# Scores of 26 expert tiles moved out of the expert loop of a two-block transformer kernel

## The reference, cut to what matters

```python
q = jnp.einsum('td,dhk->thk', x_t, w_q).reshape(T, PEER_HEADS, 2, PEER_HALF)
s = jnp.einsum('thpk,hpnk->thpn', q, sub_keys).astype(jnp.float32)
sv, si = lax.top_k(s, K)
...
fv, fpos = lax.top_k(cand, K)
eidx = jnp.take_along_axis(cidx, fpos, axis=-1)
gate = jax.nn.softmax(fv, axis=-1)
u = u_emb[eidx]
v = v_emb[eidx]
act = jax.nn.gelu(jnp.einsum('thkd,td->thk', u, x_t).astype(jnp.float32), approximate=False)
return jnp.einsum('thk,thkd->td', (gate * act).astype(x_t.dtype), v)
```

## Time and profile before

| | |
|---|---|
| median of 3 runs | 2806.69 us |
| the profiled execution, its span | 2806.97 us, 2804.9 us |
| PE, PEld busy | 2476.3 us (88%), 2096.4 us (75%) |
| DVE, ACT busy | 2020.6 us (72%), 539.7 us (19%) |
| chain that ended last | PE 77%, DVE 15%, issue 3% |
| layer 0: key choice, gate making | 665.8 to 777.7, 777.7 to 887.2 us |
| layer 0: start, experts | 887.2 to 893.8, 893.8 to 1614.3 us |
| layer 1 | the same, 1171 us later (key choice ends at 1948.7) |

### The profile page before, as it was taken

How to read it: one execution, slowest core, us unless ns; L and a number is a source line. 1 busy time by engine, 2 the same in 40 slices (tenths; PEclk the granted TensorE clock), 3 DMA queues, 4 the chain that set the end, 5 groups by cost and what they waited for, 6 DMA issues and landing times.

```text
span 2804.9 us, 40133 instructions
## 1 busy us (share of the span) xinstructions
PE 2476.3 (88%) x13930; PEld 2096.4 (75%) x13930; DVE 2020.6 (72%) x4410; ACT 539.7 (19%) x943; POOL 0.2 (0%) x4
## 2 busy tenths in 40 slices
PE   8977999788467999999999976783789999999998
PEld 6645886455456999999999955462579999999997
DVE  2334344634999888888888754469988888888887
ACT  2322000110133111111111133310321111111111
POOL 0000000000000000000000000000000000000000
PEclk9978999799789999999999988896999999999998
DMA  5323677552100555555555452011025555555553
GB/s 210 126 88 132 242 288 279 216 218 90 46 0 28 190 183 191 182 192 181 193 180 191 160 201 90 31 61 45 0 83 182 192 180 193 181 192 182 190 184 128
DMA packets 87182, 429.05 MB, mean 153 GB/s; under 512 B 10064, under 2 KB 10704, under 8 KB 77008
## 3 DMA queue, kind: packets, MB, share of 16 engines
q1 hardware_dynamic: 87120, 428.23, 43.6%
HBM read 427.14 MB, written 1.05 MB: 153 GB/s over the span
## 4 chain that ended last, share of the span: by engine, by line
PE 77%; DVE 15%; issue 3%; ACT 2%; DVEq 1%; DMA 1%; SPq 0%; ACTq 0%
PE ps L430 53%; PE ps L462 10%; PE ps L452 6%; DVE HN L1464 4%; PE ps L628 2%; PE ps L492 1%; DVEq L1464 1%; PE ps L510 1%; DVE HT L1100 1%; DVE HN L1462 1%; DVE arena L1382 1%; DVE arena L1380 1%; DVE arena L1386 1%; DVE arena L1220 1%; ACT arena L855 1%
## 5 line engine op out<-in xcount | busy, mean ns | idle before, releaser
L430 PE MATMUL ps<-ring_rounded 128*128 128x256 f32 x4096 | 778.4, 283 | 3.6 <-DVE ring_rounded L1482 3.6
L430 PE MATMUL ps<-ring_rounded,HN_rounded 128*128 128x512 f32 x3072 | 744.9, 391 | 1.3 <-DVE HN_rounded L1482 1.3
L430 PEld LDWEIGHTS ps<-ring_rounded 128*128 128x128 f32 x4096 | 656.5, 192 | 13.8 <-DVE ring_rounded L1482 4.0
L430 PEld LDWEIGHTS ps<-ring_rounded,HN_rounded 128*128 128x128 f32 x3072 | 560.6, 188 | 107.8 <-DVE HN_rounded L1482 2.0
L1482 DVE TENSOR_TENSOR ring_rounded<-ring,ring_rounded 128x1024 fp32r<-128x1024 f32 x512 | 625.4, 1222 | 9.0
L430 PE MATMUL ps<-HT_rounded,ring_rounded 128*128 128x256 f32 x2048 | 580.2, 283 | 0.0
L1478 DVE CAST ring_rounded<-ring 128x1024 fp32r<-128x1024 f32 x512 | 352.9, 689 | 213.6 <-DMA ring<-in_experts_u 211.0
L430 PEld LDWEIGHTS ps<-HT_rounded,ring_rounded 128*128 128x128 f32 x2048 | 392.8, 192 | 9.8
L462 PE MATMUL ps<-HT,ring 128*128 128x256 f32 x1472 | 335.7, 389 | 18.6 <-DVEq L1107 18.6
L462 PEld LDWEIGHTS ps<-HT,ring 128*128 128x128 f32 x1472 | 285.5, 196 | 60.8 <-DVEq L1107 20.6
L975 ACT ACTIVATE HN<-ps 128x256 f32<-128x256 f32 x256 | 98.5, 385 | 1169.7 <-PE ps L430 1169.7
(11 more groups left out here) (193 smaller groups left out, 1541.1 us busy)
## 6 DMA issues: line engine op xcount, KB each, us to landing
ring<-in_stream SPq DMA_DIRECT2D x69, 2048.0 KB, 7.7
ring<-in_experts_u SPq DMA_DIRECT2D x256, 512.0 KB, 4.4
ring<-in_experts_v SPq DMA_DIRECT2D x256, 512.0 KB, 3.7
ring<-in_stream SPq DMA_DIRECT2D x2, 1024.0 KB, 7.3
arena<-in_keys SPq DMA_DIRECT2D x2, 1024.0 KB, 14.1
ring<-in_stream SPq DMA_DIRECT2D x1, 1664.0 KB, 8.3
ring<-in_stream SPq DMA_DIRECT2D x1, 1040.0 KB, 19.3
X<-in_x SPq DMA_DIRECT2D x1, 1024.0 KB, 4.9
```

The costliest lines, as they stand in the source:

```text
L430: mm = pe.matmul(out_, p, q, start=(first and i == 0), stop=(last and i == 2))
```

## The change

Of the 128 tiles of each layer, the scores of 26 are computed ahead of the experts, by plain fp32 matmuls on the unsplit HT and u (`early_scores`): 12 behind the last key scores, 2 behind the transposes, and 12 in eighths between the groups of gate making (`gate_steps`: three matmuls in every two groups). Four slots of `ring`, then free, hold their u. ACT applies gelu and keeps the result: 14 tiles (`CHOICE_TILES`) in `early`, in the arena; 12 (`GATE_TILES`) in `meanwhile`, in `ring`. For the 14, the gates are multiplied in at once: behind the one-hots of group g, DVE multiplies the gates of group g-2, straight from PSUM, into `early` (`gate_early`), once ACT has copied the other 114 columns. The buffer of gates shrinks to 114 columns a token. The gates' exponentials and sums are now one step for all heads. The gate loops are written out. The experts begin with 26 tiles of values alone (`early_expert`); the other 102 go as before.

```diff
+P_SLOTS = 4
+CHOICE_TILES, GATE_TILES = 14, 12
+AFTER_CHOICE, AFTER_EXP = 12, 8
+EARLY = CHOICE_TILES + GATE_TILES
+LATE = TILES - EARLY
...
+def gate_steps(g):
+    every = range(GATE_TILES * KT * g // (T // GROUP), GATE_TILES * KT * (g + 1) // (T // GROUP))
+    return [(CHOICE_TILES + n, [s % KT for s in every if s // KT == n]) for n in sorted({s // KT for s in every})]
...
@@ TensorE
+                def early_scores(n, steps):
+                    if 0 in steps:
+                        pe.wait_ge(sem(f"early_u{n % P_SLOTS}_arrived"), 16 * (l * len(range(n % P_SLOTS, EARLY, P_SLOTS)) + n // P_SLOTS + 1))
+                        if n >= 2:
+                            pe.wait_ge(sem("early_kept"), l * EARLY + n - 1)
+                    for k in steps:
+                        mm = pe.matmul(ps[:, 4 + n % 2, 0:T], pre_u[:, n % P_SLOTS, k * P:(k + 1) * P], HT[:, k, :],
+                                       start=(k == 0), stop=(k == KT - 1))
+                    if KT - 1 in steps:
+                        mm.then_inc(sem("expert_scored"), 1)
+                for n in range(AFTER_CHOICE):
+                    early_scores(n, range(KT))
+                pe.wait_ge(sem("early_kept"), l * EARLY + AFTER_CHOICE)
                 pe.wait_ge(sem("chosen"), l + 1)
...
+                for n in range(AFTER_CHOICE, CHOICE_TILES):
+                    early_scores(n, range(KT))
...
+                for g in range(NG):
+                    gate_products(g)
+                    for n, steps in gate_steps(g):
+                        early_scores(n, steps)
...
+                for n in range(EARLY - 1):
+                    expert_values(n, base + n + 1, first=(n == 0))
+                expert_scores(EARLY, l * LATE + 1)
+                expert_values(EARLY - 1, base + EARLY)
@@ ScalarE
+                for g in range(NG):
+                    act.wait_ge(sem("gates_made"), l * NG + g + 1)
+                    act.activation(gates[:, g * GROUP:(g + 1) * GROUP, :], r3(ps[:, 6 + g % 2, :], GROUP)[:, :, CHOICE_TILES:], ACT.Copy)\
+                       .then_inc(sem("gates_stored"), 1)
+                    for n, steps in gate_steps(g):
+                        if KT - 1 in steps:
+                            keep_scores(n)
@@ VectorE
+                def gate_early(g):
+                    dve.wait_ge(sem("gates_stored"), l * NG + g + 1)
+                    if g == 0:
+                        dve.wait_ge(sem("early_kept"), l * EARLY + CHOICE_TILES)
+                    part = early_t[:, g * GROUP:(g + 1) * GROUP, :]
+                    dve.tensor_tensor(part, r3(ps[:, 6 + g % 2, :], GROUP)[:, :, 0:CHOICE_TILES], part, ALU.mult).then_inc(sem("gates_kept"), 1)
+                for g in range(NG):
+                    one_hots(g)
+                    if g >= 2:
+                        gate_early(g - 2)
...
+                def early_expert(n):
+                    if n < GATE_TILES:
+                        ins = dve.tensor_tensor(act_e[:, n % 2], meanwhile[:, n], gates[:, :, n], ALU.mult)
...
+                    step(high(act_h[:, n % 2], x))
...
+                    low(act_l[:, n % 2], x, act_h[:, n % 2]).then_inc(sem("expert_gated"), 1)
...
+                    v = n + 1
+                    v_arrived(v)
+                    dve.wait_ge(sem("expert_used"), base_v + n + 1)
+                    step(high(exp_vh[:, v % 2], exp_v[:, v % E_SLOTS]))
+                    settle()
+                    low(exp_vl[:, v % E_SLOTS], exp_v[:, v % E_SLOTS], exp_vh[:, v % 2]).then_inc(sem("expert_v"), 1)
@@ SyncE
+                for n in range(E_SLOTS):
+                    fetch_v(n, v[VALUES[n]])
+                for n in range(P_SLOTS, EARLY):
+                    fetch_early(n)
+                for n in range(E_SLOTS, EARLY):
+                    fetch_v(n % E_SLOTS, v[VALUES[n]], base_v + n - E_SLOTS + 2)
+                    if n == GATE_TILES + E_SLOTS:
+                        sp.wait_ge(sem("early_read"), l + 1)
+                        for j in range(EARLY, EARLY + E_SLOTS):
+                            fetch_u(j % E_SLOTS, u[j])
```

More of the change, by code:

```diff
@@ L227, in program @@
         ch = Region()
+        early = r3(ch.take(CHOICE_TILES * T), CHOICE_TILES)
+        early_t = early.rearrange("p i t -> p t i")
         pq_t = r3(ch.take(SETS * T), SETS)
@@ L676, in gate_products @@
                     mm.then_inc(sem("gates_made"), 1)
[L678 to L682, removed]
+                for g in range(NG):
+                    gate_products(g)
+                    for n, steps in gate_steps(g):
+                        early_scores(n, steps)
+                pe.wait_ge(sem("early_kept"), (l + 1) * EARLY)
                 spread(f"g2_{l}", hn_flat)
@@ L939, in experts @@
             def experts(l):
[L940 to L944, removed]
                 root(f"peer_{l}", f"mix_{l}")
@@ L953, in experts, with keep_scores @@
                         stored(f"sc_{l}_{h}")
-                    if i:
-                        gate_exp(i - 1)
-                gate_exp(3)
-                act.wait_ge(sem("slots"), 2 * l + 2)
[L960 to L966, removed]
+                def keep_scores(n):
+                    act.wait_ge(sem("expert_scored"), l * TILES + n + 1)
+                    dst = early[:, n] if n < CHOICE_TILES else meanwhile[:, n - CHOICE_TILES]
+                    act.activation(dst, ps[:, 4 + n % 2, 0:T], ACT.Gelu).then_inc(sem("early_kept"), 1)
+                for n in range(AFTER_EXP):
+                    keep_scores(n)
+                act.wait_ge(sem("gate_in"), l + 1)
+                act.activation(chosen_h[:, 2], fin_v.rearrange("p (h b) k -> p h b k", b=NB), ACT.Exp).then_inc(sem("gate_exp"), 1)
+                for n in range(AFTER_EXP, CHOICE_TILES):
+                    keep_scores(n)
+                act.wait_ge(sem("slots"), 2 * l + 2)
+                for g in range(NG):
[4 more added lines that the diff above has]
+                        if KT - 1 in steps:
+                            keep_scores(n)
                 for i in range(0, 8, 4):
@@ L1493, in experts, with u_arrived @@
                 low(ht_low, HT, ht_high).then_inc(sem("ht_split"), 1)
-                for n in range(2):
-                    arrived("u", n)
-                    step(high(exp_uh[:, n], exp_u[:, n]))
+                base = l * TILES
+                base_v = l * (TILES + 1)
+                def u_arrived(n, turn=None):
+                    count = 16 * (l * LATE // E_SLOTS + (n - EARLY) // E_SLOTS + 1)
+                    dve.wait_ge(sem(f"expert_u{n % E_SLOTS}_arrived"), count if turn is None else turn * (16 * STEP // E_SLOTS) + count)
@@ L1502, in experts @@
                 low(exp_vl[:, 0], exp_v[:, 0], exp_vh[:, 0]).then_inc(sem("expert_v"), 1)
+                dve.wait_ge(sem("g2_row"), l + 1)
+                for n in range(EARLY):
+                    early_expert(n)
                 def expert(j, turn=None, more_u=True, more_v=True):
```

181 lines of the change are left out of this document (108 added, 73 removed).

## The result

| | us, median (lowest to highest) |
|---|---|
| before, 4 runs beside | 2807.18 (2804.99 to 2807.91) |
| after, 4 runs | 2725.64 (2723.09 to 2730.53) |
| ratio of after to before | 0.9713, 95% interval 0.9696 to 0.973 |

A forecast was written before the change was run, and what follows sets the result against it. DVE was taken to bound key choice and gate making, PE the experts. +7.5 + 14.0 + 0.3 - 62.2 = -40.4 us a layer, -80.8 for two, from 2806.97 gives 2726 us; range 2698 to 2772.

The forecast's parts named there:

- third gate group later, counted from the last key scores: Key choice into gate making: DVE's third group waits for PE's early tiles, starting at 791.6 instead of 784.12, +7.5 us.
- `gate_early`, 61 groups: Gate making: the added DVE multiplication costs 0.23 us in each of 61 groups, +14.0 us a layer.
- end of gate making: End of the gate stage: one more step of the added DVE multiplication, +0.3 us a layer.
- diagonal to first values: Start of the experts: splits of HT and first v, then gating the first tile, 7.8 us in sum.
- 24 tiles of values alone and the u delay: Early experts: 12 tiles at 3.30 and 12 at 3.09 us, 76.7, plus 1.5 for u fetches.
- from the late tiles to the end: Experts from the first late tile's scores: loop as before with 24 tiles fewer at 5.62 us, 576.1 us.
- Three u tiles ... +1.5: Middle of the values alone: three u fetches make the v behind them 1 to 2 us late, +1.5 us.
- Rival 5: Key choice: PE's clock stays at 0.54, 14 tiles take 48 us more in each layer; 2823 us, chance 0.03.
- Rival 1: Values alone and gates: v lands sooner, DVE or PE set the pace, `gate_early` costs 0.10 us; 2698 us, chance 0.13.
- Rival 2: Values alone: single v fetches take 6.4 us and hold the values, +21.6 us a layer; 2769 us, chance 0.09.
- Rival 3: Gate making: `gate_early` costs as much as a PSUM copy, 0.60 us, +22.6 a layer; 2771 us, chance 0.08.
- Rival 4: Gate making: the PE, ACT, DVE round trip shows, groups take 3.1 us; slower than before, 2880 us, chance 0.05.

The follow-up runs named there:

- second profile: The changed kernel run once more as it is, with no edit, beside three variants: 2725.09 us, ratio 0.9702.
- flat_gates: Changed kernel with the early gates' multiplication on 56 neighbouring elements instead of 4 x 14 with 1 KB steps: 2719.02 us, ratio 0.9688.
- busy_pe: Changed kernel with 16 unread identity matmuls filling PE's pause ahead of the first values: 2720.58 us, ratio 0.9691.
- spread_u: Changed kernel with the three u fetches spread behind the v fetches of tiles 15, 18 and 21: 2719.07 us, ratio 0.9673.
- double_v: Changed kernel with an unread 256 KB transfer ahead of each of 19 v fetches in the values alone: 2742.78 us, ratio 0.9773.

## Why the prediction was right

**The mechanism.** The stages have the limits that it named: DVE sets the pace of gate making, PE is late at the end of key choice, the round of v's slots, with DVE only 0.1 us a tile behind it, sets that of the values alone, and PE the late tiles. The terms of a layer, forecast and measured:

| term | forecast | layer 0 | layer 1 |
|---|---|---|---|
| third gate group later, counted from the last key scores | +7.5 | +7.8 | +7.8 |
| `gate_early`, 61 groups | +14.0 | +9.6 | +9.6 |
| end of gate making | +0.3 | +0.3 | +0.2 |
| diagonal to first values | 7.8 | 7.9 | 7.9 |
| 24 tiles of values alone and the u delay | 78.2 | 83.7 (80.4 in the second profile) | 83.1 (82.7) |
| the 25th tile | 2.8 | 2.9 | 2.8 |
| from the late tiles to the end | 576.1 | 576.3 | 576.3 |
| sum, less 727.1 (729.0 in layer 1) | -40.4 | -38.6 | -41.3 |

In layer 0 the third group stands 8.54 us later by its row, but the last key scores, unchanged code, were already 0.72 us late (738.18 instead of 737.46).

**Where two terms were off, and cancelled.** `gate_early` was priced at 0.23 us: a start of 0.14, and 0.09 for the strides, from the multiplication with a strided source. It measured 0.157: 0.12 and 0.035. The strided term was over twice too large; the 0.78 ns an element came from a pair of operations that differ in more than the stride, which may be why, but this was not tested. The Trainium skill ("SBUF — State Buffer", The DMA port swizzle) has every access that crosses a 16-byte line cost extra. By flat_gates they do: 0.035 us for 56 elements read and 56 written, 0.3 ns each where 0.78 was taken. The direction agrees.

The values alone were 5.5 us longer than forecast in layer 0, and 2.2 to 4.9 in the other three stretches of the two profiles. The gate tiles took 3.31 us (922.44 to 955.58 is ten) against 3.30, the next three 3.05 against 3.09, so the steady part was right. What failed is two things beside it. "Three u tiles ... +1.5": it was 2.9 us (a step of 5.94 us from 964.73 to 970.67 where 3.09 was due), and behind this pause the clock fell and 36 matmuls took 10.34 us instead of 8.8, 1.5 more. And no term had the clock in PE's pause of 4.59 us ahead of the first values: it fell to 0.67, and two tiles took 8.94 us instead of 6.6, 2.3 more. busy_pe and spread_u take each of them away by itself, and both together bring the 24 tiles to 78.05. Behind the u wait the clock fell in the first profile and not in layer 0 of the second. Rival 5 had asked whether the clock stays low in key choice; it did not. The place to ask was the pause that the change leaves.

The landing of v was taken as 3.7 us and measured 3.4. The Trainium skill ("SBUF — State Buffer", The DMA setup-cost knee) gives an estimate of 3.2 for these 512 KB, and the measured time lies between the two. With 3.4 a round would be 9.6 us, 3.20 a tile; the gate tiles came out at 3.31, so the rest of a round, which the forecast had at 0.1 us, takes some 0.4. Part of it is v waiting for DVE, whose own time for a gate tile is 3.21 us, not 3.18; the remainder was not separated.

**Layers, unchanged code and luck.** The span fell by 82.0 us: 38.6 in the stages of layer 0, 41.3 in those of layer 1, and 2 outside them. Layer 1 gains more since the first expert tiles of the kernel before ran at a fallen clock there (0.72 in the window from 2065 to 2071 us), and its stretch from the diagonal to the end was 1.9 us longer than in layer 0; whether it does so in each run isn't known, as there is one profile of that kernel. The 2 us outside are chance: from the end of layer 0 to the last key scores of layer 1, unchanged code, it took 294.1 us before and 291.4 after, but 294.8 in the second profile of the changed kernel, and 291.3 to 297.2 in its variants. In that second profile the stages gained 41.7 and 41.2 us. So the forecast of 40.4 us a layer was near the mean, 40.7, and in part by luck: `gate_early` was put 4.4 us a layer too dear and the values alone 2 to 5.5 us too cheap, and the two errors cancelled. With only the first of them put right, the forecast would have been off by some 8 us in all.

**The rivals.** Rival 1 was right in part: `gate_early` was cheaper than forecast (0.157 us, between its 0.10 and the 0.23), and v landed sooner (3.4 us), so that DVE's own time is nearly the limit of the gate tiles; but the waits and the clock took more than this gave. Rival 2 needed landings of 6.4 us; single v tiles landed in 3.4, and even with half as much traffic again in 4.1. Rival 3 needed 0.60 us for `gate_early`. Rival 4, the one that would have been slower, needed groups of 2.51 us; they were 1.786, and removing most of PE's work there changed nothing. Rival 5 needed a clock under 1 in the key-choice tiles; it was 1.00.

## What to carry to other kernels

Work moved from where its engine is the limit to where another one is pays for itself only until that other one is done: six gate tiles a layer gave 2.4 us each, the last six choice tiles some 0.5 us each, which the runs hardly tell from nothing. A small operation on the limiting engine is to be priced by the step from start to start, here 0.16 us and not its recorded 0.25, and times the count. After such a change look for the pauses of the matmul engine that remain: here one of 4.59 us cost up to 2.3 us more in clock and one of 2.90 us 1.5 more, and filler matmuls and spaced-out fetches took them back. And two errors that cancel look like a right forecast in the total: only the stage by stage account shows them.

## What was not expected of the hardware

- The clock after a pause is not the same each time: behind the same 4.59 us, 24 matmuls took 8.47, 8.49 and 7.09 us in three profiles in which this stretch of code is the same, and 6.12 with filler. Nor does the length of the pause alone decide: behind the u fetches the clock fell after 2.90 us in the first profile (10.34 us for 36 matmuls), and in layer 0 of double_v it didn't after 3.31 us (the next tile took 2.86 us, the usual time).
- Three 512 KB fetches issued within 1 us landed 6.0 us after issue in the median, the first of them after 4.3, and the v issued 1.4 us behind the third landed after 6.6 us, 3.2 more than the 3.4 of a single one. What the burst cost was the queue ahead of the one transfer that DVE waited for.
- Recorded lengths drift while steps don't. In the changed kernel `gate_early` shows 0.25 us at 794 us and 0.32 at 901.41, and the one-hots (L1508) 0.68 and 0.74, while the groups stay 1.79 us apart. Lengths are to be compared only between neighbouring places.
- The table loads of ACT in the experts, 128 before (L975, 164.2 us in all, one in every second tile), are gone after, though ACT's work there is the same gelu; why wasn't looked into. ACT had over 1100 us of idle time, and a late tile takes the same 5.62 us of PE's time as before, so nothing shows that this moved the total; its busy time fell from 539.7 to 371.8 us mostly by it.
